# Feed-forwards of a two-layer decoder step by Strassen's algorithm, form with 15 additions, on one Trainium2 core

## The reference

```python
D_FF = ((8 * D_MODEL // 3 + 255) // 256) * 256        # 2816

def rmsnorm(x, g, eps=1e-6):
    xf = x.astype(jnp.float32)
    y = xf * lax.rsqrt(jnp.mean(xf * xf, axis=-1, keepdims=True) + eps)
    return (y * g.astype(jnp.float32)).astype(x.dtype)

def swiglu(x, wg, wu, wd):
    return (jax.nn.silu(x @ wg) * (x @ wu)) @ wd
...
        y_p = y_p + mix_p
        y_s = y_s + mix_s
        y_p = y_p + swiglu(rmsnorm(y_p, norm_ffn[layer]), ffn_gate[layer], ffn_up[layer], ffn_down[layer])
        y_s = y_s + swiglu(rmsnorm(y_s, norm_ffn[layer]), ffn_gate[layer], ffn_up[layer], ffn_down[layer])
```

## Time and profile before

| | |
|---|---|
| device time, median of 3 runs | 3591.8 us (3591.16 to 3596.52) |
| the profiled execution, first to last instruction | 3594.2 us |
| busy: TensorE, weight loads, VectorE, ScalarE, GpSimd | 3401.0, 2942.3, 1491.8, 867.6, 643.2 us |
| matmuls executed | 26991 |
| feed-forward of layer 0, of layer 1 | 1400.7 to 2202.3 us, 2792.4 to 3589.6 us |
| moved by DMA | 186.33 MB, 52 GB/s over the span |

### The profile page before, as it was taken

How to read it: one execution, slowest core, us unless ns; L and a number is a source line. 1 busy time by engine, 2 the same in 40 slices (tenths; PEclk the granted TensorE clock), 3 DMA queues, 4 the chain that set the end, 5 groups by cost and what they waited for, 6 DMA issues and landing times. The chain is left out here.

```text
span 3594.2 us, 64526 instructions
## 1 busy us (share of the span) xinstructions
PE 3401.0 (95%) x26991; PEld 2942.3 (82%) x26991; DVE 1491.8 (42%) x2726; ACT 867.6 (24%) x1649; POOL 643.2 (18%) x433
## 2 busy tenths in 40 slices
PE   8898898898989889999999998999989999999999
PEld 5666666554556579999999998888869999999999
DVE  4465666422577653323232235433433322222322
ACT  2233222111366522101011113332323211111110
POOL 0000000102100024222222213222104222212221
PEclk9999999999999989999999999999999999999999
DMA  2000000302300131111111103111122111111111
GB/s 106 19 20 11 26 8 15 125 32 70 96 2 1 68 121 60 59 58 47 45 47 40 42 29 109 36 55 67 61 91 82 54 51 36 50 36 41 53 35 67
DMA packets 77731, 186.33 MB, mean 52 GB/s; under 512 B 28412, under 2 KB 42556, under 8 KB 75468
## 3 DMA queue, kind: packets, MB, share of 16 engines
q1 hardware_dynamic: 60892, 141.85, 11.3%
q0 software_dynamic: 12272, 40.38, 3.5%
q10 hardware_dynamic: 4352, 1.05, 0.1%
HBM read 159.45 MB, written 27.92 MB: 52 GB/s over the span
## 5 line engine op out<-in xcount | busy, mean ns | idle before, releaser
L196 PE MATMUL ps<-ff_x,ff_wh 128*128 128x384 f32 (+1 forms) x3960 | 775.3, 329 | 0.0
L196 PEld LDWEIGHTS ps<-ff_x,ff_wh 128*128 128x128 f32 x3960 | 668.9, 188 | 0.8
L196 PE MATMUL ps<-ff_x,ff_wl 128*128 128x384 f32 (+1 forms) x2112 | 465.9, 329 | 0.0
L196 PEld LDWEIGHTS ps<-ff_x,ff_wl 128*128 128x128 f32 x2112 | 361.0, 188 | 0.0
L559 DVE TENSOR_TENSOR resid<-resid,ps 128x384 f32 (+1 forms) x240 | 113.3, 528 | 388.3 <-PE ps L196 388.3
L196 PE MATMUL ps<-ff_hh,ff_dh 128*128 128x384 f32 (+1 forms) x1056 | 233.6, 329 | 9.0 <-DVE ff_hl L551 4.7
L196 PE MATMUL ps<-ff_hh,ff_dl 128*128 128x384 f32 (+1 forms) x1056 | 232.9, 329 | 0.0
L196 PE MATMUL ps<-ff_hl,ff_dh 128*128 128x384 f32 (+1 forms) x1056 | 232.9, 328 | 0.0
L546 DVE TENSOR_TENSOR ff_prod<-ff_silu,ps 128x384 f32<-128x384 f32 x132 | 62.3, 528 | 349.5 <-PE ps L196 349.5
L279 POOL TENSOR_TENSOR ff_wl<-ff_w,ff_wh 128x1024 fp32r<-128x1024 f32 x44 | 111.9, 2543 | 500.4 <-ACT ff_wh L422 500.4
L196 PEld LDWEIGHTS ps<-ff_hh,ff_dh 128*128 128x128 f32 x1056 | 180.1, 188 | 10.8 <-DVE ff_hl L551 5.9
(11 more groups left out here) (611 smaller groups left out, 6164.2 us busy)
## 6 DMA issues: line engine op xcount, KB each, us to landing
ff_w<-in_wg SPq DMA_DIRECT2D x44, 512.0 KB, 3.2
ff_w<-in_wu SPq DMA_DIRECT2D x44, 512.0 KB, 3.2
ff_wd<-in_wd POOLq DMA_DIRECT2D x48, 256.0 KB, 3.0
ff_wd<-in_wd POOLq DMA_DIRECT2D x32, 320.0 KB, 3.3
rw_w<-in_w_rwkv SPq DMA_DIRECT2D x14, 512.0 KB, 3.3
ns_past<-in_cache_slc SPq DMA_DIRECT2D x48, 128.0 KB, 2.3
np_w<-in_w_nsa SPq DMA_DIRECT2D x8, 652.0 KB, 8.1
resid<-in_x SPq DMA_DIRECT2D x1, 4352.0 KB, 14.8
```

The lines of the kernel that those rows point to most:

```text
L196: mm = pe.matmul(g.ps[:, bank + c, 0:n], w[:, k, :], x[:, o:o + n], start=(first and i == 0), stop=(last and i == 2))
```

## The change

Gate, up and down are each computed as 2x2 block products by Strassen's algorithm in the form with 15 additions. The output block of a unit is two tiles of 128 rows (f = 0, 1) by two halves of the tokens (HALF = 544 columns); the inner dimension is cut in two halves, tile j with tile j + 4. Seven products take the place of eight. Each product runs over up to four inner tiles ("zones"), in the same three passes, and over two pieces of 272 columns (CHUNK). With weight blocks a11, a12, a21, a22 and seven sets made of the token blocks b:

- q0 = a11 x set 0 (b11) and q1 = a12 x set 1 (b21) make block 0;
- q2 = a22 x set 2; q3 = (a11 - a21 - a22) x set 3; q4 = (a21 + a22) x set 4; q5 = (a21 - a11) x set 5; q6 = (a12 + a11 - a21 - a22) x set 6 (b22), q3 and q5 accumulated in the bank pair of q0, q6 in that of q4, and the rest added outside PSUM.

There are 34 units per layer: gate and up in turn for 11 pairs of inner tiles (0 to 21), then 12 for down: three sub-blocks of 4, 4 and 3 pairs of inner tiles, each with the four pairs of output tiles. A unit has 7 x 4 x 3 x 2 = 168 matmuls (126 in the last four).

VectorE makes the four sums of weight blocks for each unit (L790, L735, L795) and their low parts. It makes the low parts of the sets in the first unit, together with GpSimd. The bank pairs are read by ScalarE (gate and up, copied) and VectorE (added, L810). The hidden activations of a pair are turned into their seven sets (four differences by GpSimd, L421 to L426), stored to memory in `hid` (7 x 128 x 544 per pair) and loaded again when a sub-block of down begins, since the sets of one sub-block take the place of the previous ones. Gate, up and the turned tiles live in tiles 0, 1 and 4 to 7 of `resid`, whose own contents are parked in memory during gate and up. The output projection goes through its tiles in the order 0, 4, 1, 5, 2, 6, 3, 7, and the sum of squares is kept by VectorE instead of GpSimd. All loops are written out; the three-bank pieces and `PARTS` are gone from the feed-forward. The semaphores are cleared once for reuse. In the next layer only the order of the two output weights loaded ahead changes.

Line numbers in this section are of the changed kernel, but for the rows of before. The core of the diff (signals, buffers' places and the first unit's set code are left out):

```diff
@@ -186,378 +187,728 @@
-def products(pe, g, bank, hi, lo, k, xh, xl, first, last):
...
+            def load(n):
+                if n >= 1:
+                    sp.wait_ge(summed, n)
+                for f in range(2):
+                    if n >= 1:
+                        sp.wait_ge(quarter_low[f], n)
...
+            def load_set(p, s):
+                first, k = SUBS[p]
+                sp.wait_ge(prod, 7 * (2 * PAIRS + 4 * p - 1) + s + 1)
...
+            def low_quarters(n, f):
+                k = 2 * len(zones(n))
+                pool.wait_ge(quarter_high[f], n + 1)
+                pool.tensor_tensor(ql[f][:, 0:k, :], raw[:, f, 0:k, :], qh[f][:, 0:k, :].bitcast(F32), ALU.subtract).then_inc(quarter_low[f], 1)
...
+            def product(n, q, bank, left_high, left_low, first=True):
+                last = len(zones(n)) - 1
+                if opens(n):
+                    pe.wait_ge(set_low[q], 4 + sub(n) + 1)
+                for j, z in enumerate(zones(n)):
+                    if n == 0:
+                        pe.wait_ge(set_low[q], j + 1)
+                    for x, (u, v) in enumerate(((left_high, 0), (left_low, 0), (left_high, 1))):
+                        for c in range(2):
+                            mm = pe.matmul(ps[:, bank + c, 0:CHUNK], u[:, j, :], set_of(z, v, q)[:, CHUNK * c:CHUNK * c + CHUNK],
+                                           start=(first and j == 0 and x == 0), stop=(j == last and x == 2), skip_group_check=True)
+                mm.then_inc(prod, 1)
...
+            def squares_summed():
+                pe.wait_ge(sq_added, KT - 1)
+                for c, (bank, (o, m)) in enumerate(zip((C_BANK, C_BANK + 1, B_BANK), CH)):
+                    if c == 2:
+                        pe.wait_ge(out_b, 1)
...
+                pe.wait_ge(quarter_low[0], n + 1)
+                if n == 0:
+                    pe.wait_ge(out, KT - 1)
+                else:
+                    pe.wait_ge(out_a3, n)
+                product(n, 0, A_BANK, *of(0, 0))
...
+                product(n, 2, D_BANK, *of(1, 1))
+                if n == 0:
+                    squares_summed()
+                pe.wait_ge(sum_low, 4 * n + 1)
+                pe.wait_ge(out_a1, n + 1)
+                product(n, 3, A_BANK, sh[:, 0, :, :], sl[:, 0, :, :], False)
+                pe.wait_ge(sum_low, 4 * n + 2)
...
+                product(n, 4, C_BANK, sh[:, 1, :, :], sl[:, 1, :, :])
+                pe.wait_ge(sum_low, 4 * n + 3)
+                pe.wait_ge(out_a2, n + 1)
+                product(n, 5, A_BANK, sh[:, 2, :, :], sl[:, 2, :, :], False)
+                pe.wait_ge(sum_low, 4 * n + 4)
+                pe.wait_ge(out_c1, n + 1)
+                product(n, 6, C_BANK, sh[:, 3, :, :], sl[:, 3, :, :], False)
...
+            def quarter_sums(n):
...
+                dve.tensor_tensor(to[1], a21, a22, ALU.add)
+                subtract(to[2], a21, a11)
+                dve.drain()
+                subtract(to[0], a11, to[1])
+                dve.drain()
+                dve.tensor_tensor(to[3], a12, to[0], ALU.add).then_inc(summed, 1)
...
+            def added(n, q, bank, i):
+                dve.wait_ge(prod, 7 * n + q + 1)
+                to = in_banks(block_of(n, i))
+                return dve.tensor_tensor(to, to, from_bank(bank), ALU.add)
...
+                if n + 1 < UNITS:
+                    quarter_sums(n + 1)
+                if opens(n):
+                    next_set(sub(n), 5)
...
+                if down:
+                    added(n, 2, D_BANK, 2).then_inc(out_d, 1)
                     dve.drain()
...
+                    added(n, 3, A_BANK, 1).then_inc(out_a2, 1)
```

More of the change, by code:

```diff
@@ L186, in _ @@
             pool.memset(g.mean[:, :], 1.0 / D)
[L189 to L201 removed]
+HALF = TOK // 2
@@ new lines, in output_and_feed_forward, with kind, sub, zones @@
+        loaded = lambda i: held[i] if layer == 1 and i < 2 else w[i % 2]
+        here = (so.here0, so.here1)
+        first_ready, third_ready = (1, 3, 5, 6), (2, 4, 7, 8)
+        def kind(n):
+            return ("gate", "up")[n % 2] if n < 2 * PAIRS else "down"
+        def sub(n):
+            return (n - 2 * PAIRS) // 4
+        def zones(n):
+            return range(4) if kind(n) != "down" else ZONES[sub(n)]
+        def down_pair(n):
+            return DOWN_ORDER[sub(n)][(n - 2 * PAIRS) % 4]
@@ new lines, in squares_summed @@
+            def squares_summed():
[3 more added lines that the diff above has]
+                        pe.wait_ge(out_b, 1)
+                    pe.matmul(ps[:, bank, 0:m], g.mean[:, :], sqsum[:, o:o + m], start=True, stop=True).then_inc(norm.mean_ready.sem, 1)
+            spare_products(pe, ps[:, 7, 0:256], g.mean[:, :], act_in[:, 7 * layer, 0:256], 5)
+            for i in range(KT):
+                if i == 0:
+                    early.next(pe)
+                else:
+                    pe.wait_ge(lo, i + 1)
+                if i >= 2:
+                    pe.wait_ge(out, i - 1)
+                for k in range(KT):
+                    if i == 0:
+                        both.next(pe)
+                        if k == 2:
+                            pe.wait_ge(lo, 1)
+                    mm = output_products(i, k)
+                mm.then_inc(done, 1)
@@ new lines, in _ @@
+            both.next(act, KT)
+            for i in range(KT):
+                if i + 2 < KT:
+                    high_out(i + 2)
+                if i == 2:
+                    high_quarters(0, 0)
+                    high_quarters(0, 1)
+                if i < KT - 1:
+                    square(i)
+                if i in (1, 3):
+                    j = i // 2
+                    rest(j)
+                    opening(j, 0)
+                    opening(j, 1)
+                    act.drain()
+                    for s in (4, 2, 3, 5, 6):
+                        opening(j, s)
@@ L563, in nsa_project @@
+            finish(UNITS - 1)
 def nsa_project(g, d, rw, c):
```

823 lines of the change are left out of this document (515 added, 308 removed).

## The result

The changed kernel takes 3543.8 us (median of 4 runs, 3540.4 to 3548.1) against 3591.5 us (3590.1 to 3596.5) for the kernel before beside it: a ratio of 0.9866, 95% interval 0.9852 to 0.988. It is 48 us faster, where 117 were forecast. The profiled execution has a span of 3544.1 us, against 3594.2.

What follows compares the result with a forecast made beforehand. TensorE's rate was taken to bound the feed-forwards. Per layer 693.0 + 14.9 + 23 + 6 + 2 = 738.9 us against 799.4, plus 2.9 us once, gave -118 us and a forecast of 3475 us, range 3405 to 3550.

Steps and rivals of the forecast that it cites:

- TensorE's sum: Feed-forward matmuls: 5544 per layer at 125.0 ns make 693.0 us, 99.0 less per layer if TensorE never waits.
- rival D: All feed-forward matmuls: weight loads set the pace at 272 columns, 188 ns each, making the kernel slower, 4170 us; chance 0.05.
- Gate and up units: Plain gate and up units: 21.0 us each, no added loss, covered by 1.5 us at the tight hand-over.
- thin hand-over: From q5's block to the next unit's q0: two VectorE adds, 1.45 us, fit while q6 runs 3.0 us.
- rival C: Plain units too: out_a3 comes 1.5 us late for the next unit; 1 us charged on 22 units, 3542 us; chance 0.20.
- The start: Unit 0 of each layer: VectorE's queue delays q3 and out_a3, 14.9 us above its 21.0, bounds 8 and 20.
- Openings: First down unit of each sub-block: set work overfills the shared VectorE and GpSimd port, 13 + 6 + 4 = 23 us per layer.
- Other down units: Nine down units outside openings: quarter sums share the port with GpSimd, 0.7 us each, 6 us per layer.
- Clock: TensorE at 1.2 GHz for some matmuls after long stalls: 2 us per layer.
- End of the layer: After the last matmul: both tiles of the last pair come together, 6.2 us to the mean matmul, +2.9 us once.
- Rival B: Losses vanish as VectorE gets the port and spare time swallows the rest; only the start's 8 us stay, 3398 us; chance 0.17.

Runs made afterwards that it cites:

- unit0_order: Changed kernel with unit 0 reordered: ScalarE rounds the fourth weight sum before the roots; VectorE does its low part, next quarter sums, then reciprocals; 3537.5 us.
- quarter_lows_short: Changed kernel with GpSimd computing low parts of weight quarters of units 1 to 33 for one tile only, so the product misses most of that correction; 3511.2 us.
- sums_early: Changed kernel with VectorE forming the next unit's four quarter sums at the start of each unit, except the first and the openings; 3528.3 us.
- spare_products: Changed kernel with 121 spare fp32 products per feed-forward in six of TensorE's waits, to keep its clock up; 3538.4 us.
- lows_on_vector: Changed kernel with low parts of the weight quarters of units 1 to 33 computed by VectorE instead of GpSimd; 3530.7 us.
- lows_split_set2: Changed kernel with sums_early, unit0_order and set2_on_vector's edits, and low parts of the weight quarters of units 23 and 27 on VectorE; 3503.1 us.
- recip_first: Changed kernel with VectorE's three reciprocals in unit 0 put ahead of the low part of the fourth weight sum; 3544.1 us.
- set2_on_vector: Changed kernel with hidden set 2's low part at the openings computed by VectorE right behind set 1, not by GpSimd; 3540.3 us.

## Why the prediction was wrong in size

By its own steps, per layer:

- **TensorE's sum, right.** The slot of 272 columns is 125.7 ns (units 2 to 20 take 21.11 us each, without a gap, for 168 matmuls) against 125.0 forecast, so 5544 are 696.7 us against 693.0. The rate per column of the earlier trace rows held, and rival D (weight loads) fell. The formula of the Trainium skill (TensorE: Matmul & The Clock Gate, Back-to-back issue gap), 115.8 ns here by an estimate from it, is not what these rows show. The section gives it for an isolated matmul and not for a stream in which each has its weight load, which the prediction left out.
- **Gate and up units, nearly.** 447.2 us for 21 are 3.9 above 21 x 21.11. Of these, 2.7 are in unit 1 (23.84 us), behind the long wait and at half clock at first, and 1.1 in unit 21 (22.23 us), at the hand-over to the first opening. The thin hand-over held: no wait in units 2 to 20, so rival C fell.
- **The start, wrong: 14.9 us forecast, 26.2 measured** (47.3 - 21.1), outside the bounds of 8 to 20. q3 starts at 25.5 and not 21.9; it runs 2 us long at half clock; and out_a3 comes 7.6 us after q6 and not 2.0. The step that failed put the reciprocals right behind the roots. It overlooked that low_sum(0, 3) stands ahead of them and waits for ScalarE, which does that rounding only after draining q3. unit0_order confirms the order: the wait fell to 2.98 us, 1.0 above the forecast 2.0, with two low parts stretched by the port in it. q3's lateness is read from the rows alone: ahead of the add that it waits for, four set steps of VectorE took 6.19 us beside GpSimd's set parts, where each alone takes 0.78. The forecast of the start had left the port out.

```profile
1419.65 2.57 DVE L763 SCALAR_TENSOR_TENSOR ff_sets_raw<-resid,param,ff_sets_raw 128x544 f32<-128x544 f32 x2
1422.74 3.62 DVE L772 SCALAR_TENSOR_TENSOR ff_sets<-ff_sets_raw,param,ff_sets 128x544 fp32r<-128x544 f32 x2
...
1418.28 2.66 POOL L404 TENSOR_TENSOR ff_sets<-ff_sets_raw,ff_sets 128x544 fp32r<-128x544 f32 x2 [32.25 <-ACT ff_sets L574]
1422.36 3.43 POOL L404 TENSOR_TENSOR ff_sets<-ff_sets_raw,ff_sets 128x544 fp32r<-128x544 f32 x2 [1.41 <-DVE ff_sets_raw L763]
```

- **Openings, the mis-sized term: 23 us forecast, 37.6 measured** (units 22, 26 and 30 take 95.7 us, TensorE's own time is 21.1 + 21.1 + 15.8). The mechanism was named, but the sum of the port's work over two units is not its price. It had 15.2 us over in the first opening (57.2 in 42.0) and 2.3 in the second (44.3 in 42.0), and was written down to 13 and up to 6, because what is over could slip on. Measured are 19.7 and 11.1: the work collides inside the opening, and TensorE waits there at the second, fourth and sixth product in turn, while VectorE is idle for part of the units on both sides. quarter_lows_short takes 9.3 us off the three. It leaves 28, in which no run separates GpSimd's part of the sets from the length of VectorE's own queue.
- **Other down units, nearly:** 6 forecast, 9.5 and 7.2 measured in the two layers; sums_early removes nearly all of it.
- **Clock: 2 us forecast, somewhat more measured.** TensorE's busy time is 721.75 us, 25 beyond its slots, which looks like a large loss to half clock. spare_products refuted that: with six waits filled, the feed-forwards are 3.5 and 4.0 us shorter, 2.6 of it behind unit 0. The 2 us of q3 in unit 0 are counted under the start.
- **End of the layer, right:** the mean matmul starts 6.2 us after the last product (3.3 before).

Sum of the misses: slots 3.7, unit 1's half clock beyond the forecast 0.7, hand-over to the opening 1.1, start 11.3, openings 14.6, other down units 2.4: about 34 us per layer, and the spans have 68 for two. So two steps failed: the openings were priced by a sum of work over two units, and the start without the port and by a queue order that the kernel does not have. Down by seven products therefore lost 8 and 10 us in the two layers in place of gaining 12 in the first (231 + 23 + 6 forecast, against 271.8), and the whole gain is in gate and up. Rival B fell with the port, and for late DMAs no row speaks. C's time (3542) was met by chance, without its mechanism.

The port is shown as the cause for the down units that are no openings and for 9.3 of the openings' 37.6 us: by work taken away (quarter_lows_short), by the same work at another time (sums_early) and by the same work on the other engine (lows_on_vector). For the other 28 us it is argued: even lows_split_set2 has the three openings at 90.6 us, 32.6 above TensorE's own. Open too is what the first half of unit 0 would gain by another order of its openings (waits of 2.15, 0.60, 3.56 and 5.32 us), which wasn't tried.

## What to carry to other kernels

Where two engines exclude each other, add their busy times in each stretch as if they were one engine, and look at when they collide: moving four sums by some 4.5 us gained 15 us with no work saved. A sum over a long stretch hides collisions inside it, so make it for the shortest stretch in which the work must be done. A wait that an edit removes is gained only if the engine behind it is free then; recip_first and set2_on_vector took 1.7 and 5.3 us off the wait they aimed at and gained 0 and 3.5 us for both layers together. Half clock cost most where TensorE itself set the pace afterwards (2.6 us behind unit 0, 0.9 in unit 22), so judge it by the time of the stretch and not by the busy time.
